# The residual input in two column halves around two weight quarters, and a scratch tile zeroed at the start

## The reference

```
h = rmsnorm(x, norm_g[0, 0])           # x: 256 x 1024
p = h @ ev_w_in                        # first mixer; its columns in groups: hq, hf, hi, hgate, rq, ...
f = lb + (1 - lb) * sigmoid(hf)        # gated scan (hgrn2) from silu(hq), 1 - f, log(f), hi
...
x = x + rmsnorm(y, norm_g[0, 1])       # x is also the residual
```

## Time and profile before

| what | value |
|---|---|
| median of 3 runs | 952.98 us (952.94 to 953.1) |
| profiled execution | 952.96 us, span of its instructions 950.8 us |
| granted TensorE clock, mean | 0.998 of full speed |
| PE busy | 942.6 us (99%) |
| DVE busy | 705.5 us (74%) |
| ACT busy | 544.7 us (57%) |
| read from HBM | 185.37 MB, 196 GB/s over the span |

### The profile page before, as it was taken

The page is one execution under the profiler, slowest core; times in us unless marked ns, Lnnn a source line. Parts: engine busy times, 40 slices in busy tenths (PEclk is TensorE's granted clock), DMA queues, the critical chain, the costliest instruction groups (busy, mean ns, idle before and its releaser), DMA issues.

```text
span 950.8 us, 12835 instructions
## 1 busy us (share of the span) xinstructions
PE 942.6 (99%) x5042; PEld 814.1 (86%) x5042; DVE 705.5 (74%) x962; ACT 544.7 (57%) x737; POOL 52.7 (6%) x31
## 2 busy tenths in 40 slices
PE   9999999999999999999999999999999999999997
PEld 8898888888888889988888888878888888888886
DVE  6999555778888867997778888868556888755464
ACT  7855564765544657566765544657445656535433
POOL 0000000000000001030000000000000000003000
PEclk9999999999999999999999999999999999999999
DMA  9955436377777765435477777874765444567511
GB/s 329 320 176 165 146 133 204 128 238 263 230 236 249 253 200 176 136 133 158 174 245 263 226 240 249 291 191 143 231 201 177 162 150 157 163 212 243 200 45 45
DMA packets 122911, 187.26 MB, mean 197 GB/s; under 512 B 5379, under 2 KB 88804, under 8 KB 122852
## 3 DMA queue, kind: packets, MB, share of 16 engines
q1 hardware_dynamic: 122416, 186.05, 59.6%
q10 hardware_dynamic: 436, 0.40, 0.1%
HBM read 185.37 MB, written 1.06 MB: 196 GB/s over the span
## 4 chain that ended last, share of the span: by engine, by line
PE 95%; DMA 2%; DVE 1%; ACT 1%; issue 0%; SPq 0%; DVEq 0%; ACTq 0%
PE bank L708 94%; DMA raw<-in_ev_w_in 2%; PE bank L966 1%; DVE wl L1257 1%; PE bank L1059 0%; PE bank L1136 0%; DVE hx L1263 0%; DVE arena L1767 0%; ACT wh L1938 0%; PE bank L918 0%; PE bank L770 0%; ACT arena L1933 0%; DVE arena L1257 0%; ACT scr L1933 0%; DVE lbs L1257 0%
## 5 line engine op out<-in xcount | busy, mean ns | idle before, releaser
L1257 DVE TENSOR_TENSOR wl<-raw,wh 128x2048 fp32r<-128x2048 f32 (+1 forms) x159 | 360.1, 2268 | 125.9 <-ACT wh L1938 99.8
L1938 ACT CAST wh<-raw 128x2048 fp32r<-128x2048 f32 x154 | 292.8, 1911 | 122.0 <-PE bank L708 120.0
L708 PE MATMUL bank<-hx,wh 128*128 128x512 f32 (+1 forms) x1280 | 280.6, 360 | 0.2 <-DVE wh L1302 0.2
L708 PEld LDWEIGHTS bank<-hx,wh 128*128 128x128 f32 x1280 | 223.1, 189 | 34.4 <-issue 0.9
L708 PE MATMUL bank<-wh,hx 128*128 128x512 f32 x560 | 179.8, 394 | 0.6 <-ACT hx L1933 0.5
L708 PE MATMUL bank<-wh,yh 128*128 128x512 f32 (+1 forms) x420 | 163.1, 388 | 0.0
L708 PE MATMUL bank<-wh,yl 128*128 128x512 f32 (+1 forms) x420 | 162.6, 387 | 0.0
L708 PE MATMUL bank<-wl,yh 128*128 128x512 f32 (+1 forms) x420 | 162.6, 387 | 0.0
L708 PE MATMUL bank<-hx,wl 128*128 128x256 f32 x1088 | 162.0, 284 | 0.0
L708 PEld LDWEIGHTS bank<-hx,wl 128*128 128x128 f32 x1088 | 145.7, 191 | 2.6 <-DVE wl L1257 0.2
L708 PEld LDWEIGHTS bank<-wh,hx 128*128 128x128 f32 x560 | 104.8, 188 | 23.1 <-issue 1.0
(11 more groups left out here) (209 smaller groups left out, 716.6 us busy)
## 6 DMA issues: line engine op xcount, KB each, us to landing
raw<-in_mlp_w SPq DMA_DIRECT2D x64, 1024.0 KB, 5.3
raw<-in_w_in SPq DMA_DIRECT2D x40, 1024.0 KB, 5.1
raw<-in_ev_w_in SPq DMA_DIRECT2D x18, 1024.0 KB, 5.5
raw<-in_w_ada SPq DMA_DIRECT2D x12, 1024.0 KB, 5.1
raw<-in_od_w_in SPq DMA_DIRECT2D x12, 1024.0 KB, 5.2
raw<-in_ev_w_out SPq DMA_DIRECT2D x6, 1024.0 KB, 5.0
raw<-in_od_w_out SPq DMA_DIRECT2D x4, 1024.0 KB, 4.9
raw<-in_w_o_conv SPq DMA_DIRECT2D x4, 1024.0 KB, 4.9
```

The costliest lines, as they stand in the source:

```text
L708: return eng.matmul(o, l, r, start=start, stop=stop, skip_group_check=True)
L1257: return eng.tensor_tensor(o, x, y, op)
L1938: eng.copy(part(wh, u), part(raw, u)).then_inc(S["hi"], 1)
```

## The change

There are four edits. (1) SP loads x in two halves of its columns, each for all 256 tokens, and issues the second between quarters 1 and 2 of unit 0. (2) PE transposes the rows first, then the four slabs of the first half, and the other four between the products of quarters 1 and 2; a bank is full after 4 transposes. (3) On ACT both `x_root` move behind the loop over quarters: `x_root(0, 0)` ahead of the first half of unit 1, `x_root(0, 1)` between its halves. Since the squares go over all columns of a token tile, both wait for both halves of x. (4) The memset of `wf` moves to the beginning of DVE's list.

```
--- before.py
+++ after.py
@@ -638,8 +638,12 @@
 
         @block.sync
         def _(eng):
-            eng.dma_start(x[:, 0, :], a["x"][0:P, :]).then_inc(S["d_x0"], 16)
-            eng.dma_start(x[:, 1, :], a["x"][P:2 * P, :]).then_inc(S["d_x1"], 16)
+            def residual(half):
+
+                eng.dma_start(x[:, :, half_of(half)], a["x"].rearrange("(t p) d -> p t d", p=P)[:, :, half_of(half)]).then_inc(
+                    (S["d_x0"], S["d_x1"])[half], 16)
+
+            residual(0)
             for u in range(NU):
                 if u == 3:
                     eng.dma_start(rows2[0:ROWS2, :], a["rows2"]).then_inc(S["d_small"], 16)
@@ -691,6 +695,8 @@
                     for n, landed in enumerate(pieces_landed(u)):
                         c = piece_of(u, n)
                         eng.dma_start(slot(raw, u)[:, c, :], unit_src(u)[:, c, :]).then_inc(landed, 16)
+                        if (u, n) == (0, 1):
+                            residual(1)
                 else:
                     eng.dma_start(slot(raw, u), unit_src(u)).then_inc(raw_sem[u % RING], 16)
 
@@ -715,6 +721,8 @@
                     return m
 
                 for n in range(4):
+                    if n == 2:
+                        x_turn_first(1)
                     if n == 0:
                         eng.wait_ge(S["hi_first"], 1)
                     elif n < 3:
@@ -967,17 +975,14 @@
                     if k % 4 == 3:
                         m.then_inc(S["x_t"], 1)
 
-            def x_turn_first():
-
-                for t in range(TT):
-                    if t == 1:
-                        eng.wait_ge(S["d_rows"], 16)
-                        eng.transpose(PS[2][:, 0:ROWS1], rows1[0:ROWS1, :], ident[0:ROWS1, 0:ROWS1]).then_inc(S["colsT"], 1)
-                    eng.wait_ge((S["d_x0"], S["d_x1"])[t], 16)
-                    for k in range(KT):
+            def x_turn_first(half):
+
+                eng.wait_ge((S["d_x0"], S["d_x1"])[half], 16)
+                for k in range(4 * half, 4 * half + 4):
+                    for t in range(TT):
                         m = eng.transpose(x_bank(k)[:, t * P:(t + 1) * P], x[:, t, k * P:(k + 1) * P], ident[:, :])
-                        if t == 1 and k % 2 == 1:
-                            m.then_inc(S["x_t"], 1)
+                    if k % 2 == 1:
+                        m.then_inc(S["x_t"], 1)
 
             def root_spread():
 
@@ -994,7 +999,9 @@
             eng.wait_ge(S["const"], 1)
             idle_products(4)
             eng.wait_ge(S["d_ident"], 16)
-            x_turn_first()
+            eng.wait_ge(S["d_rows"], 16)
+            eng.transpose(PS[2][:, 0:ROWS1], rows1[0:ROWS1, :], ident[0:ROWS1, 0:ROWS1]).then_inc(S["colsT"], 1)
+            x_turn_first(0)
             eng.wait_ge(S["const"], 2)
 
             def small_turn():
@@ -1406,6 +1413,7 @@
             eng.memset(ones[:, :], 1.0).then_inc(S["const"], 1)
             eng.memset(eps[:, :], EPS).then_inc(S["const"], 1)
             link(eng.memset(u_row, -MASKED))
+            link(eng.memset(wf[:, 0:1024], 0.0))
             tensor = eng.tensor_copy
             low = [col1[:, R_LOWER + HEADS * r:R_LOWER + HEADS * (r + 1)] for r in range(3)]
 
@@ -1865,9 +1873,6 @@
                     eng.wait_ge(S["f"], 1)
                     ts(g_qk[:, :, 1, :], g_b.rearrange("p (h t) -> p h t", h=HEADS), -1.0, 1.0, ALU.mult,
                        ALU.add).then_inc(S["k_hg"], 1)
-
-                    eng.wait_ge(S["hl"], KT)
-                    link(eng.memset(wf[:, 0:1024], 0.0))
                 if u == at("hq", 1):
                     wait_evac(eng, u)
                 if u == at("rgate", 3):
@@ -1971,19 +1976,19 @@
                 eng.copy(part(wh, u)[:, c], part(raw, u)[:, c]).then_inc(done, 1)
 
             def prenorm_first():
-                eng.wait_ge(S["d_x0"], 16)
-                x_root(0, 0)
                 eng.wait_ge(S["cols"], 1)
-                for n in (0, 1, 2, 3):
+                for n in range(4):
                     eng.wait_ge(S["x_t"], n + 1)
                     for k in (2 * n, 2 * n + 1):
                         act(hh[:, k, :], x_bank(k), ACT.Copy, scale=col1[:, R_NORM + k:R_NORM + k + 1]).then_inc(S["hh"], 1)
                     if n:
                         high_piece(0, n)
+                eng.wait_ge(S["d_x0"], 16)
+                eng.wait_ge(S["d_x1"], 16)
+                x_root(0, 0)
                 high_piece(1, 0)
+                x_root(0, 1)
                 high_piece(1, 1)
-                eng.wait_ge(S["d_x1"], 16)
-                x_root(0, 1)
 
             def y_squares(p, t, half):
                 wait_acc(eng, p, t, half)
```

## The result

The changed kernel takes **956.47 us** (median of 6 runs; one of them, 2447.01 us, is an outlier that the comparison leaves out) against 953.12 us before, measured on the same chip. The ratio is 1.0032, with a 95% interval of 1.0021 to 1.0043: slower by about 3.3 us, or 0.3%. I had forecast 956.2, slower. The profiled execution has a span of 954.2 us against 950.8.

What follows compares the result with a forecast made beforehand. PE, busy 99% of the span, was taken to bound the kernel. Broadcast delay +3.4 us, less 0.2 given back, made +3.2 on 952.96: 956.2 us; own range 955.2 to 957.8, overall range 954.2 to 958.2.

Steps and rivals of the forecast that it cites:

- Start of PE: First products of unit 0: rows land at 5.1, first product near 6.5 in place of 7.62, a gain of 1.1 us.
- My late bound: Latest landing of the rows at the start, 5.79 us in place of the estimated 5.1; worth +0.7 us.
- Second transposes and the wait behind them: Between quarters 1 and 2: 0.93 us of transposes in PE's queue, then a new PE wait of 1.2 us for ACT.
- Quarters 2 and 3: End of unit 0: 0.2 us of new PE waits in these quarters, behind ACT's casts and DVE.
- The roots: Unit 1 on ACT: both statistics precede the second half cast, ending 18.3 against 13.34; PE waits 0.5 + 0.7 + 0.6 us.
- Given back at 35.47: PE's single 0.17 us wait behind DVE at 35.47 goes, because DVE catches up: -0.2 us.
- the memset: DVE's 0.91 us at 31.30 move to 1.3 us, where DVE is idle: 0 gained; with PE on time 0.17.
- rival C: Pauses from 12 to 23 us drop PE to 1.2 GHz: +1.9 to +5.8 us on top, about 959; chance 0.06.
- A: At unit 1's second half cast: ACT's order isn't waited for, so not slower, 952.4 to 953.5 us; chance 0.10.
- B: Statistics overlap the casts or DVE's part is shorter; PE only 1.5 to 2.3 us late, 954.4 to 955.2; chance 0.10.
- D: Whole kernel faster by over 0.2%, needing 1.9 us, more than the whole earlier start; chance 0.02.

Runs made afterwards that it cites:

- after_again: The changed kernel run once more without any edit, as control: 955.70 us, ratio 1.0031 to the kernel before.
- after: The changed kernel with all four edits, in its first measurement and profile, against the kernel before: 956.47 us, ratio 1.0032.
- turn_early: The changed kernel with the second eight transposes one quarter earlier, between the products of quarters 0 and 1: 954.53 us, ratio 1.0013 to the kernel before.
- memset_only: The kernel before with only the memset of wf moved to the beginning of DVE's list: 952.55 us, ratio 0.9995.
- roots_only: The kernel before with only ACT's order changed, both x_root moved behind the loop over quarters: 953.77 us, ratio 1.0009.
- the two roots runs: The changed kernel with both x_root ahead of quarter 2's hh (ratio 1.0021), or behind unit 1's casts, DVE's first reciprocal next to the second (1.0019).
- before: The kernel without the change, the reference of all ratios: 953.12 us.
- before_cold: The kernel before with one idle product less at PE's start, 3 in place of 4: 953.67 us, ratio 1.0008.

## Why the prediction was right

The direction, the total (956.2 for 956.47; on the profiles 3.2 for 3.46) and most of the mechanism were right. That the total came out so near is luck: PE's start and the stalls of quarters 2 and 3 cost 1.3 and 0.4 us more than forecast in the first profile, and the roots and what is given back took about 0.8 and 0.4 off. In the second profile of the same kernel PE starts 0.9 us sooner, and its last matmul comes 2.76 us later than before in place of 3.46. My own range, too, was not the sum of my bounds: those add up to 955.7 to 958.0, where I wrote 955.2 to 957.8.

- **Start of PE: wrong by 0.4 to 1.3 us.** I had PE's first product at 6.5, a gain of 1.1; the profiles of the unedited program have 7.77 and 6.90. Two parts. The rows landed at 5.76 and 5.45, not 5.1. I had read the last packets of their queue in the trace before and taken their time for the landing. But in after_again that queue (q10) moves nothing between 4.75 and 5.45 us, and PE waits for the rows until 5.45; in after it moves nothing between 5.16 and 5.76. The wait ends 0.6 to 0.7 us behind the last packet. Only in after were the packets later than in before as well, where the last of them ended by 5.0. My late bound, 5.79, held. And in the first profile PE ran its products 0.21 us apart up to 8.9 us, at the lower level of the clock, a possibility I had considered only for the pauses behind 12 us.
- **Second transposes and the wait behind them: right.** 2.13 us forecast (0.93 + 1.2), 2.04 measured, twice (0.79 and 1.25 by turn_early); turn_early shows that it is the wait of ACT's chain, and that the place decides.
- **Quarters 2 and 3: too small.** 0.2 us forecast. Quarter 2 to broadcast costs 0.64 beyond the roots.
- **The roots: too large, and not the largest term.** I wrote under "The roots on ACT": "This is the largest term", with waits of 0.5 + 0.7 + 0.6 = 1.8 us in unit 1. Measured 0.98. My chain on ACT took 1.48 us for each root's block and 1.03 for each half; the changed kernel needs 3.72 from 14.37 to 18.09 for both blocks and the first half, where I had 4.0, and PE ended unit 0 later than I had it, so that more of ACT's time lay beside PE's work. The largest term is the wait behind the transposes, 1.25.
- **Given back at 35.47: too small.** 0.2 forecast; 0.4 to 0.8 in the profiles with the memset moved (0.6 in the first). I counted only the idle time of 0.17 us that the profile names. PE's restart behind it (35.47 to 35.80, for 0.23 between such products elsewhere) and the gap in front, covered by the modelled matmul ends, went with it: 0.44 us in all. I had valued the memset at 0 with PE late. No run has the changed kernel with the memset left in place; it speaks for the 0 that PE comes there 0.7 us after DVE is done (39.28 and 38.6), and the memset stood 0.4 in front of the scans. With PE in time I had said 0.17 and no more, and memset_only's profile has more than that.
- **The clock behind 12 us (rival C): did not happen.** After pauses of about 1 us the products from quarter 2 on are 0.12 us apart, and the granted clock stays at 1.00, the level of 2.4 GHz, until behind the last matmul. The Trainium skill ("TensorE: Matmul & The Clock Gate", section "HAM oscillation — how this bites in real kernels") warns of waiting phases between bursts of matmuls, but of longer ones than any here. By that section these pauses cost nothing, and the trace agrees.
- **Rivals A, B and D** did not come about; roots_only and the two roots runs speak against A at its own place.

## What to carry to other kernels

When work is moved into a stream of products, don't price the work alone: look at which engine starts on its result, and how long that engine then needs until the stream can go on. Here 0.8 us of transposes cost 2.0 us, and at a place one weight quarter earlier they cost 0.8. Price a block on one engine by how much of it stands outside waits that are already there, since terms on two engines overlap and their sum can be right for the wrong reasons; the distance between two fixed instructions in several profiles separates them better than total times do.

## What was not expected of the hardware

The same program on the same inputs can run its first products at either of two rates. Eight 128 x 128 transposes at the start took 1.09 us in one profile of a list and 1.86 in another with the same list on PE (before, memset_only), and 1.91 and 1.04 us in two profiles of the changed kernel. From start to start that is 0.21 us against 0.11, close to the ratio of TensorE's two clock levels (1.2 and 2.4 GHz), and the change of rate falls on the first entry of the trace's clock record: at 4.85 us, before the first transpose, in before; at 6.58, between its two sets, in memset_only; at 8.91 and 3.84 in the two profiles of the changed kernel; at 9.92 in before_cold. The views print the granted clock as 1.00 ahead of that entry as well, so there the spacing of the products tells the rate and the column does not. It moves the first product by 0.4 us (memset_only against before) to 0.8 (before_cold against before), as much as the edits that were to be told apart.
